# Two blocks on one Trainium2 core: second output tile begun later, score fills moved, inverse roots in pairs, some probability scalings on ScalarE

## What is computed

```python
h = rms_norm(x, norm1_g)
glu_in, q, k, v, gate_logits = split(h @ w_in)
a = silu(rms_norm(causal_conv31(a_val * sigmoid(a_gate))))
q, k = rms_norm_per_head(q), rms_norm_per_head(k)      # 16 heads of 64
o = softmax(q k^T - slopes * dist, dilated windows) @ v
x = x + (g_a * (a @ w_conv_out) + g_b * (o @ w_attn_out)) @ w_out
x = x + (silu(u_gate) * u_val) @ w_down                # u = conv3(rms_norm(x) @ w_up)
# second block
score = sum over 8 index heads of relu(qi ki^T) * wi   # top 128 keys of each row
y = (softmax(q k^T over the chosen keys) @ v * silu(g)) @ w_out_a
x = layer_norm(ALPHA * x + y)
y = (stick_breaking(q, k) @ v * silu(g)) @ w_out_b     # exp(log_sigmoid(z) + reverse cumsum)
x = layer_norm(ALPHA * x + y)
```

## Time and profile before

| | |
|---|---|
| time, median of 3 | 1543.39 us (1543.38 to 1544.44) |
| profiled execution, its own time | 1542.46 us |
| its span | 1540.5 us |
| PE busy | 1515.3 us, 98% |
| DVE, ACT, POOL busy | 1152.0, 887.0, 768.8 us |
| HBM read | 199.75 MB, 131 GB/s over the span |
| granted clock, mean | 0.998 |

### The profile page before, as it was taken

How to read it: one execution, slowest core, us unless ns; L and a number is a source line. 1 busy time by engine, 2 the same in 40 slices (tenths; PEclk the granted TensorE clock), 3 DMA queues, 4 the chain that set the end, 5 groups by cost and what they waited for, 6 DMA issues and landing times.

```text
span 1540.5 us, 21821 instructions
## 1 busy us (share of the span) xinstructions
PE 1515.3 (98%) x7792; PEld 1293.6 (84%) x7792; DVE 1152.0 (75%) x2064; ACT 887.0 (58%) x1544; POOL 768.8 (50%) x726
## 2 busy tenths in 40 slices
PE   9999999999999999999999999999999999999997
PEld 7888899988888888888888888887888988888877
DVE  5999999998664687437717559967777828988977
ACT  6445788787433344324324464689995327777753
POOL 2232345435465477557747563456655424444443
PEclk9999999999999999999999999999999999999999
DMA  7889765665332222323222278856457945456551
GB/s 222 194 186 203 165 137 130 146 161 126 123 107 91 91 96 96 110 83 110 96 96 89 96 180 188 177 130 140 110 126 177 202 106 132 109 123 137 109 121 59
DMA packets 60299, 203.26 MB, mean 132 GB/s; under 512 B 6816, under 2 KB 9376, under 8 KB 60192
## 3 DMA queue, kind: packets, MB, share of 16 engines
q0 software_dynamic: 19008, 69.21, 26.3%
q1 hardware_dynamic: 40896, 132.14, 25.8%
q10 hardware_dynamic: 288, 0.52, 0.1%
HBM read 199.75 MB, written 2.10 MB: 131 GB/s over the span
## 4 chain that ended last, share of the span: by engine, by line
PE 84%; DVE 7%; ACT 5%; DMA 2%; issue 1%; POOL 1%; DVEq 0%; SPq 0%; POOLq 0%; ACTq 0%
PE bank L368 82%; PE bank L374 2%; DVE r L407 1%; DMA w_raw<-in_weights 1%; ACT k_both L378 1%; ACT prob L378 1%; ACT w_hi L378 1%; DVE pt_lo L395 1%; DMA w_lo<-in_weights 1%; DVE prob L1288 0%; ACT pt_hi L378 0%; DVE r L395 0%; DVE q_both L407 0%; DVE score L1875 0%; ACT soft L378 0%
## 5 line engine op out<-in xcount | busy, mean ns | idle before, releaser
L414 POOL TENSOR_TENSOR w_lo<-w_raw,w_hi 128x512 fp32r<-128x512 f32 (+1 forms) x190 | 278.5, 1485 | 210.3 <-ACT w_hi L378 210.3
L378 ACT ACTIVATE w_hi<-w_raw 128x1024 fp32r<-128x1024 f32 (+2 forms) x206 | 213.9, 1041 | 278.7 <-PE bank L368 253.3
L368 PE MATMUL bank<-x_hi,w_hi 128*128 128x512 f32 x872 | 346.6, 398 | 1.3 <-DVE k_lo_first L407 0.6
L368 PE MATMUL bank<-x_hi,w_lo 128*128 128x512 f32 x872 | 340.6, 391 | 0.6 <-DMA w_lo<-in_weights 0.4
L368 PE MATMUL bank<-x_lo,w_hi 128*128 128x512 f32 x872 | 340.1, 390 | 0.0
L368 PEld LDWEIGHTS bank<-x_hi,w_lo 128*128 128x128 f32 x872 | 163.7, 188 | 37.0 <-POOL w_lo L414 0.8
L368 PEld LDWEIGHTS bank<-x_hi,w_hi 128*128 128x128 f32 x872 | 163.9, 188 | 33.4 <-ACT k_both L378 1.0
L368 PEld LDWEIGHTS bank<-x_lo,w_hi 128*128 128x128 f32 x872 | 164.2, 188 | 29.8
L621 POOL DMA_DIRECT2D w_lo<-in_weights x132 | 117.0, 894 | 120.4 <-ACT w_lo L378 96.3
L368 PE MATMUL bank<-a_hi,w_hi 128*128 128x512 f32 x416 | 162.0, 389 | 0.0
L368 PE MATMUL bank<-a_hi,w_lo 128*128 128x512 f32 x416 | 161.8, 389 | 0.0
(11 more groups left out here) (230 smaller groups left out, 3403.5 us busy)
## 6 DMA issues: line engine op xcount, KB each, us to landing
w_raw<-in_weights SPq DMA_DIRECT2D x223, 512.0 KB, 3.4
w_lo<-in_weights POOLq DMA_DIRECT2D x132, 512.0 KB, 6.6
alibi<-in_alibi SPq DMA_DIRECT2D x16, 256.0 KB, 3.9
w_raw<-in_weights SPq DMA_DIRECT2D x8, 384.0 KB, 3.0
r<-in_x SPq DMA_DIRECT2D x8, 256.0 KB, 6.1
r<-in_x SPq DMA_DIRECT2D x4, 512.0 KB, 6.2
out_y<-r SPq DMA_DIRECT2D x16, 128.0 KB, 1.8
w_raw<-in_weights ACTq DMA_DIRECT2D x2, 256.0 KB, 4.2
```

The source lines that it names most:

```text
L368: return e.matmul(out, lhsT, rhs, start=start, stop=stop, skip_group_check=resumed)
L378: return self.act.run(lambda e: e.activation(out, in_, func, **kw), after, 0.07 + size(out) * 0.00086 + 0.09 * len(kw))
L414: return self.pool.run(lambda e: e.tensor_tensor(out, a, b, op), after, cost)
```

## The change

Five things are changed.

1. `two_tiles`, while heads are woven in: the first tile runs four units ahead of the second (`LEAD`), and the second tile takes its weights and its bank only when its first unit comes. It touches the last pair of gate tiles in the first mixer, and the first pairs of `attn_out`, `out_a` and `out_b`.
2. The fills of `score` and `select` are taken out of `index_scores` and made a stream of their own, `blank_scores`, which is due behind the last user of the hidden layer.
3. `rsqrt` keeps g = m*y beside y in one tile and updates both in one instruction of twice the width: 8 DVE instructions for 10.
4. The ones of the column sums are 1/1024, so that scaling by it falls away; `half_norm` has one small instruction fewer.
5. In the first mixer a scaling of probabilities is planned on ACT when ACT's planned time is earlier than POOL's.

```diff
+LEAD = 4
...
-        for key in keys:
-            begin(key)
-        for k in range(n_k - 1):
+        ahead = LEAD if self.in_heads else 0
+        order = sorted(((k, n) for k in range(n_k - 1) for n in range(len(keys))), key=lambda u: (u[0] if u[1] else u[0] - ahead, u[1]))
+        for k, n in order:
             while known is not None and k not in known and self.in_heads:
                 yield "idle"
-            for c, b in zip(cs, bs):
-                tok = self.unit(c, b, k, hi, lo, ready, False, used is not None and c == cs[-1])
-                if used is not None and c == cs[-1]:
-                    used[k] = [tok]
-                self.tick()
-                yield
+            while n == len(cs):
+                begin(keys[n])
+            second = used is not None and n == len(keys) - 1
+            tok = self.unit(cs[n], bs[n], k, hi, lo, ready, False, second)
+            if second:
+                used[k] = [tok]
+            self.tick()
+            yield
...
-    def rsqrt(self, m, y, t, ready):
+    def rsqrt(self, m, gy, t, ready):
+        g, y = gy[:, 0, :], gy[:, 1, :]
         tok = self.v_ts(y.bitcast(I32), m.bitcast(I32), -0.5, MAGIC, ALU.mult, ALU.add, [ready])
-        for _ in range(3):
-            tok = self.v_tt(t, y, y, ALU.mult, [tok])
-            tok = self.v_stt(t, t, -0.5, m, ALU.mult, ALU.mult, [tok])
-            tok = self.v_stt(y, t, 1.5, y, ALU.add, ALU.mult, [tok])
+        tok = self.v_tt(g, m, y, ALU.mult, [tok])
+        both = t.rearrange("p (o n) -> p o n", o=1).to_broadcast([P, 2, t.shape[-1]])
+        for n in range(3):
+            tok = self.v_stt(t, g, -0.5, y, ALU.mult, ALU.mult, [tok])
+            if n < 2:
+                tok = self.v_stt(gy, both, 1.5, gy, ALU.add, ALU.mult, [tok])
+            else:
+                tok = self.v_stt(y, t, 1.5, y, ALU.add, ALU.mult, [tok])
         return tok
...
-        tok = self.v_ts(m, b.ap[:, 0:NT], 1.0 / D, eps, ALU.mult, ALU.add, [tok])
+        tok = self.v_ts(m, b.ap[:, 0:NT], eps, None, ALU.add, after=[tok])
         b.release([tok])
-        tok = self.rsqrt(m, y, t, tok)
+        tok = self.rsqrt(m, gy, t, tok)
...
+        self.pair_m, self.pair_t = self.cols(16), self.cols(16)
+        self.pair_gy = self.cols(32).rearrange("p (a n) -> p a n", a=2)
...
-        self.ones_ready = self.v_fill(self.ones, 1.0)
+        self.ones_ready = self.v_fill(self.ones, 1.0 / D)
...
-        tok = self.rsqrt(mean, y, w, tok)
+        tok = self.rsqrt(mean, self.pair_gy, w, tok)
...
-                ready[i] = self.p_ts(pr, pr, self.row_inv[s][:, i:i + 1], 0.0, ALU.mult, ALU.add, [inv, self.exps[h][i]])
+                scale, after = self.row_inv[s][:, i:i + 1], [inv, self.exps[h][i]]
+                if self.norm_by_act(h, i):
+                    ready[i] = self.a_op(pr, pr, ACT.Copy, after, scale=scale)
+                else:
+                    ready[i] = self.p_ts(pr, pr, scale, 0.0, ALU.mult, ALU.add, after)
             self.p_ready[h] = ready
         self.start(steps())
+    def norm_by_act(self, h, i):
+        return self.finish == self.first_o and self.act.time < self.pool.time
...
-    def index_scores(self):
+    def blank_scores(self):
+        yield self.hid_used
+        yield 4.0
         t0 = self.v_fill(self.score[:, :], 0.0, self.hid_used)
         for i in range(1, NT):
             a = self.SOFF[i] + P * i
             t0 = self.v_fill(self.score[0:64, a + 64:a + P], -BIG, [t0])
-        tok = {i: t0 for i in range(1, NT)}
         t1 = self.v_fill(self.select[:, 0:P], 0.0)
         self.select_ready[0] = [self.v_fill(self.select[0:64, 64:P], BIG, [t1])]
+        self.blank[0] = t0
+    def index_scores(self):
+        t0 = self.got(self.blank, 0)
+        tok = {i: t0 for i in range(1, NT)}
...
+        self.blank = {}
+        self.start(self.blank_scores())
...
-        t1 = self.v_ts(mu, b.ap[:, 2 * half:2 * half + 2], 1.0 / D, None, ALU.mult, after=[t])
-        t2 = self.v_ts(m, b.ap[:, NT + 2 * half:NT + 2 * half + 2], 1.0 / D, None, ALU.mult, after=[t])
-        b.release([t2])
-        t = self.v_tt(w, mu, mu, ALU.mult, [t1])
-        t = self.v_tt(m, m, w, ALU.subtract, [t2, t])
+        t1 = self.v_copy(mu, b.ap[:, 2 * half:2 * half + 2], [t])
+        w_done = self.v_tt(w, mu, mu, ALU.mult, [t1])
+        t = self.v_tt(m, b.ap[:, NT + 2 * half:NT + 2 * half + 2], w, ALU.subtract, [t, w_done])
+        b.release([t])
```

## The result

The changed kernel takes 1548.35 us (median of 7 runs, 1547.13 to 1549.71) against 1543.46 for the kernel before in the same comparison: a ratio of 1.0031, interval 1.0022 to 1.0040. The forecast was 1541.2, the range 1538.3 to 1543.4. It went to the slower side, by a mechanism that was not the slower rival's.

A forecast was written before the change was run, and what follows sets the result against it. PE, busy 98%, was taken as the bound, leaving 25.2 us of idle time to win. Terms 0.25 + 0.25 + 0 + 1.5 + 0.15 = 2.15 us took 1543.4 to 1541.2; 8-in-10 range 1538.3 to 1543.4.

The forecast's parts named there:

- the slower rival: First mixer: scalings on ACT hold up its in-order queue and PE waits; 4.4 us slower, 1547.8, chance 0.08.
- The first mixer: Reordered engines there win 1.5 us: three stalls give 2.4, less 0.9 of new waits; bounds 0 to 3.5.
- (b): First mixer, head 4: of PE's 1.6 us wait for POOL's `prob`, 0.9 us won.
- (a): First mixer at 177.84 us: of the 1.32 us stall for `k_lo_first`, about 1.0 won.
- (c): First mixer, 330 to 400 us: of PE's 0.87 us idle time, 0.5 won.
- 0.9 of new ones: First mixer: 0.9 us of new waits made by moved instructions, chosen between 0 and 2.4.
- Stick mixer's end: The 2.45 us wait for `r` goes, but most returns as a wait for `o_lo`; 0.25 us won, of 0 to 1.4.
- k = 7: Unit at the stick mixer's end: PE waits there for `o_lo`, since the units behind PV end 1.37 us sooner.
- the last head's own chain does not move: Stick mixer's end: head 15's sums, PV and `o_lo` keep their times though units are brought forward.
- Sparse mixer's end: Of the 0.78 us stall for `o_lo`, 0.5 returns as a wait at unit k = 6; 0.25 won, of 0 to 0.78.
- Fills: Moved into DVE's idle time they cost nothing; the 1.56 us wait at the sparse heads' start stays; 0 won, of 0 to 1.6.
- Norms: Shorter inverse roots and `half_norm` on PE's path, mostly hidden: 0.15 us won in all.

The follow-up runs named there:

- e3: The changed kernel with head 4's first scaling also on ACT; the planner then made another order, with 22 scalings on ACT: 1544.58 us, 1.0012.
- e4: The changed kernel without the lead (LEAD = 0), both tiles of a pair in turn from the start, as before the change: 1551.37 us, 1.0052.
- e14: The changed kernel, every engine's order kept, with one more wait in each of seven convolution steps behind head 4's reciprocal, making small gaps: 1544.24 us, 1.0001.
- e2: The changed kernel with the old inverse root of ten instructions, scalings on ACT kept (22 of 64): 1543.53 us, 1.0006.
- e10: The changed kernel with a planner rule: in the first mixer no third convolution step in a row on DVE while POOL has planned work: 1553.78 us, 1.0065.
- e8: The kernel before with only the column sums by 1/1024 and the shorter half norm: 1543.90 us, 1.0001.
- e13: The kernel before plus a block behind its last store: POOL scaling beside DVE steps, with subtraction, DMA, matmuls or ACT work; scaling 0.92 or 0.36 to 0.38 us.
- e5: The kernel before plus a block behind its last store: a POOL scaling beside plain two-input DVE steps; scaling 0.37 us alone, 1.42 beside two to eight.
- e6: The kernel before plus a block behind its last store: a POOL scaling beside steps of the convolution's form or with parts left out; scaling 0.38 to 1.42 us.
- e9: The kernel before with the early fills alone: 1543.10 us, 0.9997.
- e11: The changed kernel with the planner rule against a third convolution step in a row, and the later second tile in the first mixer only: 1550.94 us, 1.0046.
- e12: The changed kernel with all scalings on POOL and the later second tile in the first mixer only: 1542.07 us, 0.9989.
- e7: The kernel before with the later second tile alone: 1543.28 us, 1.0004.
- e1: The changed kernel with all 64 scalings of the first mixer on POOL again: 1543.01 us, 1.0002.

## Why the prediction was wrong

**The first mixer is the step that failed**, in its part (b): "They are still all POOL's in this head, and the same convolution steps on DVE lie beside them", from which I took 0.9 us of gain, of 0 to 1.6. The row it stood on, 5.46 us for four scalings, of which the first took 3.17 beside four steps, was already the mechanism, and the changed order has seven steps there. So "the same convolution steps" was false, and with it the term: PE's waits for `prob` there are 3.09 us now (2.13 + 0.96) instead of 1.6, a loss of 1.5 where I had a gain of 0.9, and the low clock comes on top. Had I read 3.17 us as four steps' length and counted the steps in the new order, I would have had some 2 us of loss there (an estimate from those rows). I left a loss out of the bounds altogether. Part (a) came out at 0.75 of the 1.0: the wait of 1.32 is 0.57 now, for `k_both`. Part (c) came out in full: PE has no idle time from 330 to 400. The "0.9 of new ones" was mis-sized: the stall for `pt_lo` alone is 2.21.

**The clock** was in no term and no rival. PE's instructions took 2.9 us longer in that stretch, of its 5.4, and about half of that is the fall at 196 us that e3, e4 and e14 don't have.

**The slower rival** named the wrong thing. ACT's scalings cost PE nothing that shows: e2 has 22 of them at 1.0006, and e10 idles least with 21.

**Stick mixer's end**: right that the 2.45 us wait goes and comes back elsewhere. k = 7 waits for `o_lo` 1.08 us, where I expected 1.4. Wrong that "the last head's own chain does not move": `sp_lo` is waited for 1.06 us instead of 0.48, and in the order the last head's scores stand behind the five units brought forward, which I take for the reason (no run tests it, and the same wait is 0.90 to 0.95 in the kernels of the old order whose clock falls ahead of it). The term was +0.25 and came out as -0.77 to -0.81 in each kernel with the later tile, measured against a profile of before in which the clock stayed at 1.00. That was one of two cases. Of the nine profiles with the old order of `out_b`, the clock stays at 1.00 behind the stall of 2.45 us in three (before, e8, e13) and falls in six (e4, e5, e6, e9, e11, e12; in e9 it is 0.82 from 1465 to 1471 us), which makes the stretch 2.0 to 3.5 us longer; e5, e6 and e13 are the same kernel. In all seven later-tile profiles taken it stays at 1.00. So the later tile loses 0.8 us against the one case and wins 1.2 or more against the other.

**Sparse mixer's end**: right. k = 6 waits for `o_lo`, 0.38 us (0.5 expected), for the 0.78 to 0.80 of all but one of the profiles without the later tile (e5 has 0.33), which is 0.4 gained for 0.25. What I had not looked at is the norm behind it, +1.3.

**Fills**: right that they cost nothing. The wait at the sparse heads' start was not fixed as I said, but e7 shows it shorter without the fills, and e5, e6 and e13 without any edit.

**Norms**: 0.15 expected; e8 shows nothing either way.

## What to carry to other kernels

Where a planner fills an engine's spare time with small pieces of a long job, look at the length of the unbroken runs that it makes, not at the engine's load: another engine that shares a path can be shut out for the whole run, and a small gap between pieces can be cheaper than a reordering (e14 took back 4 us, e10 lost 5 more). Judge a change of costs in such a planner by counting the runs in the new order at the places where the trace shows an operation stretched already. An edit that is harmless without another (e1, e2) can be bad together with it, since both move the same plan. And take more than one profile of the kernel before: three repeats, here a by-product of blocks behind the last store, showed which stretches repeat within 0.12 us and which move by 1 to 2 us by themselves.

## What the runs showed of the hardware

- A POOL scaling of 128x128, 0.37 us by itself, took 2.02, 2.69, 3.17 and 5.15 us beside unbroken runs of two, three, four and seven two-input DVE steps, and one of 128x256 (0.47) 4.12 beside five; where several runs have the same place, they agree within 0.01 us. It took 1.11 where the steps started 0.77 us apart instead of 0.66. Beside other steps of the same kernels, such as head 0's, it was not shut out. In blocks of the same form behind the kernel (e5, e6, e13) it took 0.36 to 1.42. Why the block's runs let it through is open.
- The granted clock fell to 0.50 for about 3 us behind PE stalls of 1.8 us and more in some executions and not in others: the `pt_lo` stall of 2.2 us has it in the changed kernel (196 to 198 us at 0.50) and not in e3, e4 and e14 (1.00), and the stall of 2.45 us at the stick mixer's end has it in e5 and e6 and not in e13, which are one and the same kernel up to there. It cost 1.5 us behind the first and 2.0 behind the second.
